# Two attentions of a streaming encoder: the two heads of a pair issued in turn, with one pair of logits ahead of the transposes

## The chip, the cores and the metric

The kernel runs on one core of one Trainium2 chip. The metric is the device time of one execution in microseconds (us). The core has five engines with instruction streams of their own, which meet only through semaphores: TensorE (PE in the profile, with PEld for its weight loads) does matmuls and transposes and writes to PSUM; VectorE (DVE) and ScalarE (ACT) read PSUM and do elementwise work and reductions; GpSimd (POOL) does elementwise work in SBUF; SyncE (SP) issues the loads.

## The reference

Two layers of an encoder are applied to a prompt of 512 frames and to a sample of 32 frames with 256 cached ones; the width is 1024. Layer 0 mixes by two gated recurrences, layer 1 by two attentions of 8 heads of 64 each: a forgetting attention (FoX) with causal masking and a decay added to the logits, and an attention over the keys that an indexer selects (DSA, 2 key heads shared by 4 query heads each). Each layer ends in a gated feed-forward network.

```python
def fox_attention(q, k_all, v_all, logf_all, q_start):
    ...
    def block(args):
        qb, cqb, pb = args
        logits = jnp.einsum('bqhd,bshd->bhqs', qb, k_all).astype(F32) * (hd ** -0.5)
        logits = logits + cqb.transpose(0, 2, 1)[..., None] - cum_t[:, :, None, :]
        logits = jnp.where(key_pos[None, None, None, :] <= pb[None, None, :, None], logits, -jnp.inf)
        p = jax.nn.softmax(logits, axis=-1)
        return jnp.einsum('bhqs,bshd->bqhd', p.astype(v_all.dtype), v_all)
...
def dsa_attention(q, k_all, v_all, iq, iw, ik_all, q_start):
    ...
        score = jax.nn.relu(jnp.einsum('bqhd,bsd->bqhs', iqb, ik_all).astype(F32))
        score = jnp.einsum('bqhs,bqh->bqs', score, iwb.astype(F32)) * IDX_SCALE
        ...
        _, idx = lax.top_k(score, topk)
        ...
        logits = jnp.einsum('bqgnd,bqkgd->bqgnk', qg, k_sel).astype(F32) * (hd ** -0.5)
        logits = jnp.where(valid[:, :, None, None, :], logits, -jnp.inf)
        p = jax.nn.softmax(logits, axis=-1)
        o = jnp.einsum('bqgnk,bqkgd->bqgnd', p.astype(v_sel.dtype), v_sel)
...
def run_trunk(...):
    for layer in range(DEPTH):
        xn = rmsnorm(x, norm_mix[layer])
        ...
        x = x + y
        x = x + swiglu(rmsnorm(x, norm_ffn[layer]), ffn_w_in[layer], ffn_w_out[layer])
```

All inputs and outputs are float32.

## The kernel before

Nearly all of the program is weight streaming: `plan` cuts every weight matrix into chunks of 128x1024; SyncE loads them into four slots, ScalarE makes the high part (`w_hi`), GpSimd the low part (`w_lo`), and TensorE multiplies three products of high and low parts (`job`, `tm_section`). Activations lie transposed, features on the partitions and the 544 frames (512 and 32) along the free axis. The order of every engine's instructions is written out by hand in one function per engine.

The change touches the function `attention(dsa)` alone, which stands once in each of three engines' programs (ScalarE, TensorE, VectorE) and is called twice in each: `attention(0)` for FoX and, after five jobs for DSA's keys and queries, `attention(1)` for DSA. Selection is done by adding a mask of large negative numbers, so both attentions have the same form.

The work of an attention is cut into `groups`. Group x belongs to a head h = 2t+e. Heads 2t and 2t+1 are a pair: their queries `qT[:, t, :]` and (in FoX) keys lie in partitions 0 to 63 (e=0) and 64 to 127 (e=1) of the same tile. A head has three groups: the first holds two query tiles of 128 rows, with 128 and 256 keys, side by side in one PSUM bank; the second one query tile with 384 keys; the third one with 512. Two more groups hold the 32 sample frames, four heads each (`tiles` is None). NX = 26 groups in all.

For a group the engines do in turn:
- `masks` (TensorE): decay and causal mask, or the selection's mask, as bf16 matmuls into logits bank x % 4. It waits until the exponentials of group x-4 are done (`at_e`).
- `logits` (TensorE): query times key added on top, float32. Signals `at_l`.
- `maxima` (VectorE): the row maxima. Signals `at_mx`.
- `exps` (ScalarE): exponentials with row sums into `prob[:, x % 3]`. Signals `at_e`.
- `normalise` (VectorE): reciprocal of the sums and scaling. Signals `at_p`.
- `turn` (TensorE): transposes of 128x128 into bank 4 + x % 2. Signals `at_t`.
- `copies` (ScalarE): that bank into the SBUF buffer `pt[x % 2]`. It waits for `at_t` and, since the buffer must be free, for the values of group x-2 (`at_v`). Signals `at_c`.
- `values` (TensorE): value times transposed probabilities. Even heads give rows 0 to 63 and odd heads rows 64 to 127 of bank 6 or 7. Signals `at_v`.
- `outputs` (ScalarE, then VectorE): once per pair of heads, the result as high and low part.

Before the change TensorE's loop over x issues masks(x+3), turn(x), logits(x+3), values(x-1); ScalarE's issues exps(x+2), copies(x); VectorE's issues maxima(x+2), normalise(x+1). In `attention(0)` VectorE also has rounds of the indexer's search (`largest`, `replace`) between the groups x = 1 to 5. The two buffers of `pt` are shown as `m_only` and `arena` in the profile.

## Time and profile before

| | before |
|---|---|
| time, median of 3 runs | 1521.56 us (1519.2 to 1530.3) |
| span of the profiled execution | 1520.4 us |
| TensorE busy | 1467.3 us (97%) |
| VectorE busy | 557.5 us (37%) |
| ScalarE busy | 561.3 us (37%) |
| GpSimd busy | 518.1 us (34%) |
| attention(0), first mask to last value | 882.41 to 954.16 us |
| attention(1), first mask to last value | 987.73 to 1055.30 us |

The profiled execution has no time of its own beside its span; the median of the runs is 1.2 us above that span. A busy TensorE counts from a matmul's start to its modelled end, so the distance between the starts of consecutive blocks tells better than the durations what a block costs. PEclk is the granted clock of TensorE as a share of 2.4 GHz; it has two levels, 1.00 and 0.50.

### The profile page before, as it was taken

How to read it: one execution, taken by the hardware profiler on the slowest of the kernel's cores; microseconds unless marked ns; L12 is line 12 of the kernel's file. 1: busy time of each engine (PE TensorE's matmuls, PEld its weight loads, DVE VectorE, ACT ScalarE, POOL GpSimd, SP SyncE). 2: the span in 40 equal slices, each digit the busy share in tenths (PEclk: the TensorE clock that was granted, in tenths of full speed). 3: DMA queues.
4: the chain of work that ended last, by engine and by line, in shares of the span. 5: the costliest groups of instructions: out<-in, count | busy, mean ns of one | idle time of the engine just before them, and what ended most of it. 6: DMA issues, size and time to landing. Idle time of an engine off the chain costs nothing.

```text
span 1520.4 us, 27440 instructions
## 1 busy us (share of the span) xinstructions
PE 1467.3 (97%) x11103; PEld 1361.9 (90%) x11103; DVE 557.5 (37%) x1131; ACT 561.3 (37%) x907; POOL 518.1 (34%) x235
## 2 busy tenths in 40 slices
PE   4998999999999999999999999999999999999998
PEld 3777889899999999999988766957999999999997
DVE  5114536633421223122408975163343212221224
ACT  4424546444432233122464254153353323321222
POOL 1421212233644344434535210300334533443442
PEclk9999899999999999999999999999999999999999
DMA  4221122232323222322332320200223332232221
GB/s 141 84 70 45 44 60 59 64 105 77 93 87 111 69 83 86 108 69 66 95 95 70 85 58 1 70 8 15 77 77 97 97 97 70 83 110 70 80 73 59
DMA packets 208777, 114.37 MB, mean 75 GB/s; under 512 B 16693, under 2 KB 202937, under 8 KB 208697
## 3 DMA queue, kind: packets, MB, share of 16 engines
q1 hardware_dynamic: 203448, 109.50, 25.0%
q10 hardware_dynamic: 5248, 3.73, 0.8%
q8 instruction: 59, 0.97, 0.3%
q14 instruction: 22, 0.17, 0.0%
HBM read 107.26 MB, written 5.96 MB: 74 GB/s over the span
## 4 chain that ended last, share of the span: by engine, by line
PE 62%; issue 29%; POOL 7%; DVE 2%; ACT 0%; POOLq 0%; DVEq 0%; ACTq 0%
PE ps L966 52%; POOL w_lo L523 7%; PE ps L1061 4%; PE ps L1283 1%; PE ps L1317 1%; PE ps L1296 1%; PE ps L1266 0%; DVE arena L1732 0%; DVE arena L1751 0%; DVE arena L1768 0%; PE ps L1312 0%; PE ps L1413 0%; DVE m_only L1763 0%; PE ps L1209 0%; DVE arena L1871 0%
## 5 line engine op out<-in xcount | busy, mean ns | idle before, releaser
L523 POOL TENSOR_TENSOR w_lo<-w_raw,w_hi 128x1024 fp32r<-128x1024 f32 x202 | 498.6, 2472 | 964.0 <-ACT w_hi L583 964.0
L966 PE MATMUL ps<-x_hi,w_hi 128*128 128x272 f32 (+1 forms) x1952 | 411.8, 293 | 10.3 <-DVE arena L1592 6.1
L966 PE MATMUL ps<-x_hi,w_lo 128*128 128x272 f32 (+1 forms) x1952 | 408.4, 291 | 0.0
L966 PE MATMUL ps<-x_lo,w_hi 128*128 128x272 f32 (+1 forms) x1952 | 407.1, 290 | 0.0
L966 PEld LDWEIGHTS ps<-x_hi,w_hi 128*128 128x128 f32 (+1 forms) x1952 | 310.5, 190 | 17.6 <-issue 11.7
L966 PEld LDWEIGHTS ps<-x_lo,w_hi 128*128 128x128 f32 (+1 forms) x1952 | 310.4, 191 | 0.5
L966 PEld LDWEIGHTS ps<-x_hi,w_lo 128*128 128x128 f32 (+1 forms) x1952 | 308.3, 191 | 0.5
L583 ACT ACTIVATE w_hi<-w_raw 128x1024 fp32r<-128x1024 f32 x202 | 211.2, 1050 | 194.2 <-PE ps L966 144.5
L966 PE MATMUL ps<-o_hi,w_hi 128*128 128x272 f32 x960 | 200.1, 290 | 2.0 <-DVE arena L1651 1.1
L966 PE MATMUL ps<-o_hi,w_lo 128*128 128x272 f32 x960 | 199.8, 290 | 0.0
L966 PE MATMUL ps<-o_lo,w_hi 128*128 128x272 f32 x960 | 199.0, 289 | 0.0
L966 PEld LDWEIGHTS ps<-o_hi,w_hi 128*128 128x128 f32 x960 | 152.0, 190 | 2.6 <-issue 2.6
L966 PEld LDWEIGHTS ps<-o_lo,w_hi 128*128 128x128 f32 x960 | 151.9, 190 | 0.0
L966 PEld LDWEIGHTS ps<-o_hi,w_lo 128*128 128x128 f32 x960 | 150.8, 190 | 0.0
L639 ACT ACTIVATE o_hi<-arena 128x544 f32 x44 | 29.0, 658 | 197.2 <-DVE arena L1504 197.2
L1497 DVE TENSOR_TENSOR arena<-ps,rstd 128x544 f32<-128x544 f32 x44 | 31.9, 725 | 163.2 <-PE ps L966 150.3
L635 ACT ACTIVATE arena<-arena 128x544 f32<-128x544 f32 x44 | 29.0, 660 | 168.6 <-DVE arena L1497 168.6
L1519 DVE TENSOR_TENSOR xT<-ps,xT 128x544 f32 x32 | 23.2, 725 | 162.9 <-PE ps L966 162.9
L1504 DVE TENSOR_TENSOR arena<-arena,ps 128x544 f32<-128x544 f32 x44 | 31.7, 721 | 123.9 <-PE ps L966 123.7
L1061 PE MATMUL ps<-w_hi,x_hi 128*128 128x512 f32 (+3 forms) x160 | 64.5, 403 | 8.1 <-DVE x_lo L1442 5.2
L1061 PE MATMUL ps<-w_hi,x_lo 128*128 128x512 f32 (+3 forms) x160 | 63.8, 399 | 0.0
L1061 PE MATMUL ps<-w_lo,x_hi 128*128 128x512 f32 (+3 forms) x160 | 63.5, 397 | 0.0
(240 smaller groups left out, 1377.4 us busy)
## 6 DMA issues: line engine op xcount, KB each, us to landing
w_raw<-in_ffn_w_in SPq DMA_DIRECT2D x88, 512.0 KB, 3.8
w_raw<-in_ffn_w_out SPq DMA_DIRECT2D x32, 512.0 KB, 3.8
w_raw<-in_ab_w_in SPq DMA_DIRECT2D x28, 512.0 KB, 3.8
w_raw<-in_cd_w_in SPq DMA_DIRECT2D x13, 512.0 KB, 3.8
w_raw<-in_ffn_w_out SPq DMA_DIRECT2D x16, 384.0 KB, 3.3
w_raw<-in_ab_w_out SPq DMA_DIRECT2D x8, 512.0 KB, 3.5
arena<-in_x_prompt SPq DMA_DIRECT2D x4, 512.0 KB, 5.0
w_raw<-in_cd_w_in SPq DMA_DIRECT2D x8, 256.0 KB, 3.5
```

The lines of the kernel that those rows point to most:

```text
L523: pool.tensor_tensor(wl[:, s, :], raw[:, s, :], wh[:, s, :].bitcast(F32), ALU.subtract).then_inc(lo_done, 1)
L583: act.activation(wh[:, s, :], raw[:, s, :], ACT.Copy).then_inc(hi_done, 1)
L635: act.activation(fsig[:, k // 2, :], fg[:, k // 2, :], ACT.Sigmoid).then_inc(f_sig, 1)
L639: act.activation(oh[:, bass.ds(i * 2 + k // 2, 1), :], fh[:, k // 2:k // 2 + 1, :], ACT.Copy).then_inc(f_hi, 1)
L966: mm = pe.matmul(ps[0:M, b + h, 0:HALF], w[:, s, k * M:(k + 1) * M], xs[x][:, k, h * HALF:(h + 1) * HALF], start=(begin and k == ks[0] and ...
L1061: mm = pe.matmul(out, (xh, xl)[x][:, k, i * P:min(T, (i + 1) * P)], w[:, s, kk * N:(kk + 1) * N], start=(k == 0 and a == 0), stop=(k == KT ...
L1283: mm = pe.matmul(L[:, c:c + nk], q[:, i * P:(i + 1) * P], ks_[:, 0:nk], start=False, stop=True, skip_group_check=True)
L1296: mm = pe.transpose(ps[0:m, 4 + x % 2, c:c + P], prob[:, x % 3, c:c + m], ident[:, :])
L1317: mm = pe.matmul(out[:, i * P:(i + 1) * P], v[:, kb, vcol], pt[x % 2][:, c + kb * P:c + (kb + 1) * P], start=(kb == 0), stop=(kb == i), sk ...
L1497: dve.tensor_tensor(two(fgk), pair(g), two(rstd[:, :]), ALU.mult).then_inc(frees(g), 1)
L1504: dve.tensor_tensor(two(fh[:, k, :]), two(fgk), pair(u), ALU.mult).then_inc(frees(u), 1)
L1519: dve.tensor_tensor(xv, pair(c), xv, ALU.add).then_inc(frees(c), 1)
```

## The change

`groups` is ordered by shape first and head of the pair last, so that groups 2s and 2s+1 are the same shape of heads 2t and 2t+1. Each engine's loop runs over the NS = 13 pairs of groups s. `logits` and `values` take a pair and issue the two heads' matmuls in turn; `masks`, `turn`, `maxima`, `exps`, `normalise` and `copies` are unchanged and are called for one head and then the other. TensorE issues masks of pair s+1, turn of pair s, logits of s+1, values of s-1. PSUM banks and buffers are the same, and so is the number of matmuls.

```diff
@@ -431,10 +431,11 @@
         N_M0_OUT = sum(2 * (1 if kind == "a" else 2) for kind, _ in units)
 
 
-        groups = [(2 * t + e, tiles) for t in range(4) for e in range(2)
-                  for tiles in ([(0, 0, P), (1, P, 2 * P)], [(2, 0, 3 * P)], [(3, 0, 4 * P)])]
+        groups = [(2 * t + e, tiles) for t in range(4)
+                  for tiles in ([(0, 0, P), (1, P, 2 * P)], [(2, 0, 3 * P)], [(3, 0, 4 * P)]) for e in range(2)]
         groups += [(w, None) for w in range(2)]
         NX = len(groups)
+        NS = NX // 2
         pairs_end = [6 * (t + 1) - 1 for t in range(4)] + [NX - 1]
         block = ctx.enter_context(nc.Block())
 
@@ -860,13 +861,15 @@
 
                 exps(0)
                 exps(1)
-                for x in range(NX + 2):
-                    if x + 2 < NX:
-                        exps(x + 2)
-                    if x < NX:
-                        copies(x)
-                    if x - 2 in pairs_end:
-                        outputs(x - 2)
+                for s in range(NS + 1):
+                    for x in (2 * s, 2 * s + 1):
+                        if s < NS:
+                            copies(x)
+                    if 2 * s - 1 in pairs_end:
+                        outputs(2 * s - 1)
+                    for x in (2 * s + 2, 2 * s + 3):
+                        if x < NX:
+                            exps(x)
 
             hp[0] = C_M1 + LEAD
             for c in range(C_M1, C_M1 + 4):
@@ -1267,22 +1270,28 @@
                                 mm = pe.matmul(L[:, o + i * P:o + nk], identb[:, :], caus, start=False, stop=False, skip_group_check=True)
                     mm.then_inc(at_m, 1)
 
-                def logits(x):
-                    h, tiles = groups[x]
-                    L = ps[:, x % 4, :]
-                    pe.wait_ge(at_m, X0 + x + 1)
-                    for k, t, e, ks_, kc_, _, o in heads_of(x):
-                        q = qT[e * HD:(e + 1) * HD, t, :]
-                        if tiles is None:
-                            pe.matmul(L[o:o + 32, 0:PAST], q[:, TP:T], kc_, start=False, stop=True, skip_group_check=True,
-                                      tile_position=(e * HD, o))
-                            mm = pe.matmul(L[o:o + 32, PAST:KS], q[:, TP:T], ks_[:, TP:T], start=False, stop=True,
-                                           skip_group_check=True, tile_position=(e * HD, o))
-                        else:
-                            for i, c, nk in tiles:
-                                mm = pe.matmul(L[:, c:c + nk], q[:, i * P:(i + 1) * P], ks_[:, 0:nk], start=False, stop=True,
-                                               skip_group_check=True)
-                    mm.then_inc(at_l, 1)
+                def logits(s):
+
+                    pe.wait_ge(at_m, X0 + 2 * s + 2)
+                    tiles = groups[2 * s][1]
+                    if tiles is None:
+                        for x in (2 * s, 2 * s + 1):
+                            L = ps[:, x % 4, :]
+                            for k, t, e, ks_, kc_, _, o in heads_of(x):
+                                q = qT[e * HD:(e + 1) * HD, t, :]
+                                pe.matmul(L[o:o + 32, 0:PAST], q[:, TP:T], kc_, start=False, stop=True, skip_group_check=True,
+                                          tile_position=(e * HD, o))
+                                mm = pe.matmul(L[o:o + 32, PAST:KS], q[:, TP:T], ks_[:, TP:T], start=False, stop=True,
+                                               skip_group_check=True, tile_position=(e * HD, o))
+                            mm.then_inc(at_l, 1)
+                        return
+                    for i, c, nk in tiles:
+                        for x in (2 * s, 2 * s + 1):
+                            (k, t, e, ks_, _, _, _), = heads_of(x)
+                            mm = pe.matmul(ps[:, x % 4, c:c + nk], qT[e * HD:(e + 1) * HD, t, i * P:(i + 1) * P], ks_[:, 0:nk],
+                                           start=False, stop=True, skip_group_check=True)
+                            if i == tiles[-1][0]:
+                                mm.then_inc(at_l, 1)
 
                 def turn(x):
 
@@ -1296,40 +1305,50 @@
                         mm = pe.transpose(ps[0:m, 4 + x % 2, c:c + P], prob[:, x % 3, c:c + m], ident[:, :])
                     mm.then_inc(at_t, 1)
 
-                def values(x):
-
-                    pi = [n for n, last in enumerate(pairs_end) if x <= last][0]
+                def values(s):
+
+                    x0 = 2 * s
+                    pi = [n for n, last in enumerate(pairs_end) if x0 <= last][0]
                     if pi + PX >= 2:
                         pe.wait_ge(at_o, PX + pi - 1)
-                    pe.wait_ge(at_c, X0 + x + 1)
-                    tiles = groups[x][1]
-                    for k, t, e, _, _, vcol, o in heads_of(x):
-                        out = ps[e * HD:(e + 1) * HD, 6 + (PX + pi) % 2, :]
-                        if tiles is None:
-                            for kb in range(3):
-                                vv = v[0:TS, NT, vcol] if kb == 2 else vc_[:, kb, vcol]
-                                m = TS if kb == 2 else P
-                                mm = pe.matmul(out[:, t * TS:(t + 1) * TS], vv, pt[x % 2][0:m, kb * P + o:kb * P + o + TS],
-                                               start=(kb == 0), stop=(kb == 2), skip_group_check=True)
-                        else:
-                            for i, c, nk in tiles:
-                                for kb in range(i + 1):
-                                    mm = pe.matmul(out[:, i * P:(i + 1) * P], v[:, kb, vcol], pt[x % 2][:, c + kb * P:c + (kb + 1) * P],
-                                                   start=(kb == 0), stop=(kb == i), skip_group_check=True)
-                    mm.then_inc(at_v, 1)
-
-                for x in range(3):
-                    masks(x)
-                    logits(x)
-                for x in range(NX + 1):
-                    if x + 3 < NX:
-                        masks(x + 3)
-                    if x < NX:
-                        turn(x)
-                    if x + 3 < NX:
-                        logits(x + 3)
-                    if x >= 1:
-                        values(x - 1)
+                    pe.wait_ge(at_c, X0 + x0 + 2)
+                    bank = 6 + (PX + pi) % 2
+                    tiles = groups[x0][1]
+                    if tiles is None:
+                        for x in (x0, x0 + 1):
+                            for k, t, e, _, _, vcol, o in heads_of(x):
+                                for kb in range(3):
+                                    vv = v[0:TS, NT, vcol] if kb == 2 else vc_[:, kb, vcol]
+                                    m = TS if kb == 2 else P
+                                    mm = pe.matmul(ps[e * HD:(e + 1) * HD, bank, t * TS:(t + 1) * TS], vv,
+                                                   pt[x % 2][0:m, kb * P + o:kb * P + o + TS],
+                                                   start=(kb == 0), stop=(kb == 2), skip_group_check=True)
+                            mm.then_inc(at_v, 1)
+                        return
+                    for i, c, nk in tiles:
+                        for kb in range(i + 1):
+                            for x in (x0, x0 + 1):
+                                (k, t, e, _, _, vcol, _), = heads_of(x)
+                                mm = pe.matmul(ps[e * HD:(e + 1) * HD, bank, i * P:(i + 1) * P], v[:, kb, vcol],
+                                               pt[x % 2][:, c + kb * P:c + (kb + 1) * P],
+                                               start=(kb == 0), stop=(kb == i), skip_group_check=True)
+                                if i == tiles[-1][0] and kb == i:
+                                    mm.then_inc(at_v, 1)
+
+                masks(0)
+                masks(1)
+                logits(0)
+                for s in range(NS + 1):
+                    if s + 1 < NS:
+                        masks(2 * s + 2)
+                        masks(2 * s + 3)
+                    if s < NS:
+                        turn(2 * s)
+                        turn(2 * s + 1)
+                    if s + 1 < NS:
+                        logits(s + 1)
+                    if s >= 1:
+                        values(s - 1)
 
             def turn_keys(src, base):
 
@@ -1806,23 +1825,20 @@
                         b = b[:, 0:4 * TS].rearrange("p (t n) -> p t n", t=4)
                     dve.tensor_tensor(o, b, hh.bitcast(F32), ALU.subtract).then_inc(at_o, 1)
 
-                maxima(0)
-                maxima(1)
-                normalise(0)
-                for x in range(NX + 3):
-
-                    late = 3 if not dsa and 1 <= x <= LATE else None
+                for s in range(NS + 2):
+
+                    late = 3 if not dsa and 1 <= s <= LATE else None
                     if late is not None:
                         largest(late)
-                    if x + 2 < NX:
-                        maxima(x + 2)
-                    if x + 1 < NX:
-                        normalise(x + 1)
-                    if x - 3 in pairs_end:
-                        outputs(x - 3)
+                    for step in (maxima, normalise):
+                        for x in (2 * s, 2 * s + 1):
+                            if s < NS:
+                                step(x)
+                    if 2 * s - 3 in pairs_end:
+                        outputs(2 * s - 3)
                     if late is not None:
                         replace(late)
-                        if x == LATE:
+                        if s == LATE:
                             chosen(late)
 
             LATE = 5
```

TensorE around the middle of attention(0), before, two groups of one head (384 and 512 keys). L1266 and L1267 are masks, L1296 transposes of the group before, L1283 logits, L1317 values:

```order
L1266 MATMUL ps<-arena 128x384
L1267 MATMUL ps<-arena,identb 128x128
L1296 MATMUL ps<-ident,arena 128x128 x3
L1283 MATMUL ps<-arena 128x384
L1317 MATMUL ps<-m_only,arena 64x128 x3
L1266 MATMUL ps<-arena 128x512
L1267 MATMUL ps<-arena,identb 128x128
L1296 MATMUL ps<-ident,arena 128x128 x4
L1283 MATMUL ps<-arena 128x512
L1317 MATMUL ps<-arena 64x128 x3
```

The same place in the changed kernel: masks (L1269, L1270) of both heads, transposes (L1305) of the pair before, logits (L1291) of both heads, values (L1332) in turn:

```order
L1269 MATMUL ps<-arena 128x384
L1270 MATMUL ps<-arena,identb 128x128
L1269 MATMUL ps<-arena 128x384
L1270 MATMUL ps<-arena,identb 128x128
L1305 MATMUL ps<-ident,arena 128x128 x6
L1291 MATMUL ps<-arena 128x384 x2
L1332 MATMUL ps<-arena 64x128
L1332 MATMUL ps<-m_only,arena 64x128
L1332 MATMUL ps<-arena 64x128
L1332 MATMUL ps<-m_only,arena 64x128
L1332 MATMUL ps<-arena 64x128
L1332 MATMUL ps<-m_only,arena 64x128
```

Before, the transposes ahead of a group's logits belong to a group two places earlier than the last logits issued; now they belong to the pair whose logits were issued last, and the values that follow belong to the pair before that one.

ScalarE at the same stage, before. L848 are copies, L832 exponentials, L856 outputs; the names in brackets are the semaphores that an instruction waits for (att_values is `at_v`, att_turned `at_t`, att_max `at_mx`):

```order
L848 ACTIVATE arena<-ps 128x384 [waits att_values,att_turned]
L832 ACTIVATE arena,small<-ps,small 128x384 [waits att_turned,att_max]
L848 ACTIVATE m_only<-ps 128x512 [waits att_values,att_turned]
L832 ACTIVATE arena,small<-ps,small 128x512 [waits att_turned,att_max]
L848 ACTIVATE arena<-ps 128x384 [waits att_values,att_turned]
L832 ACTIVATE arena,small<-ps,small 128x128 [waits att_turned,att_max]
L832 ACTIVATE arena,small<-ps,small 128x256
L848 ACTIVATE m_only<-ps 128x384 [waits att_values,att_turned]
L856 ACTIVATE o_hi<-ps 128x512 [waits att_values]
```

And in the changed kernel (L849 copies, L833 exponentials, L857 outputs):

```order
L849 ACTIVATE arena<-ps 128x512 [waits att_values,att_turned]
L849 ACTIVATE m_only<-ps 128x512 [waits att_values,att_turned]
L833 ACTIVATE arena,small<-ps,small 128x128 [waits att_turned,att_max]
L833 ACTIVATE arena,small<-ps,small 128x256
L833 ACTIVATE arena,small<-ps,small 128x128 [waits att_turned,att_max]
L833 ACTIVATE arena,small<-ps,small 128x256
L849 ACTIVATE arena<-ps 128x384 [waits att_values,att_turned]
L849 ACTIVATE m_only<-ps 128x384 [waits att_values,att_turned]
L857 ACTIVATE o_hi<-ps 128x512 [waits att_values]
L833 ACTIVATE arena,small<-ps,small 128x384 [waits att_turned,att_max] x2
L849 ACTIVATE arena<-ps 128x384 [waits att_values,att_turned]
L849 ACTIVATE m_only<-ps 128x384 [waits att_values,att_turned]
```

Copies and exponentials alternated by group; now two copies stand ahead of the exponentials of the next pair. The copies' wait for att_values was for values that TensorE issued ahead of that group's transposes; now it is for values that TensorE issues behind the next pair's logits.

## Rows read from the trace of the kernel before

**Rows 1.** The page: busy us (share of the span) and instructions of each engine.

```profile
PE 1467.3 (97%) x11103; PEld 1361.9 (90%) x11103; DVE 557.5 (37%) x1131; ACT 561.3 (37%) x907; POOL 518.1 (34%) x235
```

**Rows 2.** Windows by stage: length, busy us (instructions) of PE, PEld, DVE, ACT, POOL; PEclk.

```profile
882.41:954.16 71.75, 71.58 (x471) 45.29 (x471) 40.91 (x140) 35.40 (x101) 0.00 (x0) 0.98 0.05 17
...
987.73:1055.30 67.57, 66.63 (x430) 42.19 (x431) 37.08 (x125) 34.78 (x102) 0.00 (x0) 0.99 0.02 5
```

**Rows 3.** Timeline of PE, one head in attention 0: start, us, instructions.

```profile
901.45 0.92 PE L1283 MATMUL ps<-arena 64*128 64x128 f32 x4
902.30 1.09 PE L1317 MATMUL ps<-m_only,arena 128*64 128x128 f32 x8
...
903.98 0.91 PE L1283 MATMUL ps<-arena 64*128 64x384 f32 x2
904.82 0.87 PE L1317 MATMUL ps<-arena 128*64 128x128 f32 x6
...
905.90 0.60 PE L1296 MATMUL ps<-ident,arena 128*128 128x128 f32 x4
906.44 1.12 PE L1283 MATMUL ps<-arena 64*128 64x512 f32 x2
```

**Rows 4.** Windows of one head's cycle in each stage, columns as in rows 2.

```profile
900.73:908.29 7.56, 7.56 (x47) 4.72 (x47) 4.68 (x16) 4.22 (x12) 0.00 (x0) 1.00 0.01 2
1005.31:1012.62 7.31, 7.31 (x44) 4.57 (x43) 4.61 (x15) 4.21 (x12) 0.00 (x0) 1.00 0.00 1
```

**Rows 5.** Timeline of PE, the indexer's scores.

```profile
824.22 1.99 PE L1224 MATMUL ps<-arena 64*128 64x512 f32 x8
```

**Rows 6.** Timeline of PE, state updates with two heads and with one.

```profile
126.66 2.59 PE L1117 MATMUL ps<-arena 32*64 32x128 f32 x64
...
217.01 2.81 PE L1117 MATMUL ps<-arena 32*128 32x128 f32 x32
```

**Rows 7.** Timeline of DVE in attention 0.

```profile
907.60 0.69 DVE L1784 TENSOR_REDUCE small<-ps 128x1 f32<-128x512 f32 x1 [0.66 <-PE ps L1283]
...
908.58 0.42 DVE L1794 TENSOR_SCALAR arena<-arena,small 128x384 f32<-128x384 f32 x1
...
910.70 0.15 DVE L1791 RECIPROCAL small<-small 128x1 f32<-128x1 f32 x1
910.89 0.49 DVE L1794 TENSOR_SCALAR arena<-arena,small 128x512 f32<-128x512 f32 x1
...
913.34 0.55 DVE L1794 TENSOR_SCALAR arena<-arena,small 128x128 f32<-128x128 f32 x2
```

**Rows 8.** Timeline of ACT in attention 0.

```profile
908.51 0.69 ACT L832 ACTIVATE arena<-ps,small 128x512 f32<-128x512 f32 x1 [1.37 <-DVE small L1786]
909.09 0.19 ACT L832 ACTIVATION_READ_ACCUMULATOR arena<-ps,small 128x1 f32 x1
...
910.83 0.37 ACT L832 ACTIVATE arena<-ps,small 128x128 f32<-128x128 f32 x1 [1.16 <-DVE small L1786]
...
911.54 0.20 ACT L832 ACTIVATION_READ_ACCUMULATOR arena<-ps,small 128x1 f32 x1
911.64 0.49 ACT L848 ACTIVATE arena<-ps 128x384 f32<-128x384 f32 x1
...
913.27 0.59 ACT L832 ACTIVATE arena<-ps,small 128x384 f32<-128x384 f32 x1 [1.13 <-DVE small L1786]
...
914.10 0.60 ACT L848 ACTIVATE m_only<-ps 128x512 f32<-128x512 f32 x1 [0.17 <-PE ps L1296]
```

**Rows 9.** Windows around two falls of the clock, columns as in rows 2.

```profile
149.00:153.00 4.00, 1.71 (x14) 1.46 (x13) 1.63 (x3) 3.16 (x11) 0.00 (x0) 1.00 0.14 33
153.00:156.00 3.00, 3.00 (x15) 3.00 (x15) 0.38 (x1) 2.97 (x7) 0.00 (x0) 0.50 0.00 0
835.70:842.50 6.80, 6.06 (x14) 4.37 (x15) 6.70 (x26) 2.29 (x3) 4.71 (x2) 0.50 0.22 59
843.00:849.00 6.00, 6.00 (x28) 4.57 (x26) 5.29 (x17) 1.06 (x1) 1.35 (x1) 1.00 0.43 89
```

## The prediction

> **What bounds the kernel now.** I read the page's line of busy times first: TensorE is busy 1467.3 of 1520.4 us, VectorE and ScalarE 37% each [rows 1]. So the question is what the change does to TensorE's time, and only in the two attention stages, since everything else keeps its instructions. The windows by stage say that attention 0 takes 71.75 us and attention 1 takes 67.57, TensorE busy in 71.58 and 66.63 of them, VectorE in 40.91 and 37.08, ScalarE in 35.40 and 34.78 [rows 2]. The stages are bound by TensorE's own stream. The two steady cycles say the same: one head costs 7.56 us in attention 0 and 7.31 in attention 1, with TensorE busy throughout [rows 4]. A pair of heads therefore costs 15.12 and 14.62.
>
> The timeline of such a cycle gives the blocks [rows 3]. I call the three query groups of a head A (two tiles, 128 and 256 keys), B (384 keys) and C (512). Logits take .85 in A and .84 in B (start to next start); in C a span of 1.12, less the .07 by which a span overlaps what follows, so 1.05. Values take .87 until done, 1.09 in C (.80 and 1.02 of TensorE's time). Transposes take .54 in C, which has four, and an estimated .43 in A and B, which have three. Per head that is 2.74 for logits, 2.62 for values and 1.40 for transposes; the remaining .80 of 7.56 are masks (.55 of 7.31 in attention 1).
>
> **Part 1: pairs of matmuls.** The logits of a head contract over 64 partitions, the even head's in the lower half and the odd head's in the upper, and now follow each other tile by tile. The indexer's scores already stand so: four 64x128 matmuls of 512 columns, halves alternating, take 1.99 us [rows 5], where one alone takes 1.12 [rows 3]. So two run at once and a pair costs what one does. The values fill 64 columns of the array, even and odd head in different ones. The recurrence shows that case: 64 records of 64 columns, two heads alternating, take 2.59; 32 records of 128 columns take 2.81 [rows 6]. So these double up too. The saving on TensorE's stream is 2.74+2.62 = 5.36 per pair of heads, and with eight pairs in both stages 42.9 us. The sample groups keep their order within a head.
>
> The Trainium skill, "TensorE: Matmul & The Clock Gate", Part 3 (Packing small matmuls), gives 3.07x for four row tiles, some 77% of ideal. By it a pair would cost 1.3 times one, and TensorE's saving would shrink to an estimated 30 us. The rows here show the full factor of two, so they decide.
>
> **Part 2: the order, and what is late next.** TensorE's order is now: masks of pair s+1, transposes of pair s, logits of s+1, values of s-1. Before, logits ran three groups ahead of the transposes and the softmax of a group was hidden behind two others. Now the logits of s+1 stand behind both transposes of s, and these wait for the softmax of s. Only values and masks lie between.
>
> A second wait makes it longer. ScalarE copies the transposes of s out (`copies`) only once the values of s-1 are done, since they free that buffer; those values now stand behind the logits of s+1. On ScalarE the exponentials of s+1 are queued behind these copies. TensorE, in turn, waits for those exponentials through `normalise`. So a closed chain sets each step: logits(s+1), values(s-1), two copies of s, two groups of exponentials of s+1, the last normalise, the last transposes of s+1, next logits. The maxima of s+1 on VectorE run beside values and copies and are hidden (less than 1.7 us for two groups, against 1.7 to 2.4 of cover).
>
> The prices, from the timelines of VectorE and ScalarE: a wait between engines .04 (logits end at 906.44+1.12, the maximum starts at 907.60) [rows 3, 7]. Reciprocal to scaling .19, scaling .49 in C, .42 in B, .55 in A, with two waits: .76, .69, .82 [rows 7]. Exponentials to the end of the read-out: .91 in A, with the next ScalarE operation .81 after the start; .67 and .57 in B; .77 and .67 in C [rows 8]; B's read-out is taken as C's, .08 beyond the activation's end. A copy takes .49 (.60 in C), the next operation starting .10 before its end, as there [rows 8].
>
> A step in which the logits are A's, behind copies of C and values of B: .85 logits + .87 values + .04 + 1.00 copies + .81+.91 exponentials + .82 normalise + .43 transposes = 5.73. With B's logits: .84 + 1.09 + .04 + .78 + .50 (the pair's `outputs`, which stands there on ScalarE, priced as a copy of 512) + .57+.67 + .69 + .43 = 5.61. With C's: 1.05 + .87 + .04 + .78 + .67+.77 + .76 + .54 = 5.48. A pair of heads costs 16.8 us, against 15.12 and 14.62 now. That is +1.7 and +2.2, four times each: +15.6. Filling the pipe costs an estimated 1.5 more in both stages together: the masks of two heads stand ahead of the first logits, and the first softmax has nothing beside it. The ends, with the sample groups, I take as equal. VectorE's extra search rounds in attention 0 (`largest`, `replace`) and its `outputs` fall into the transposes and logits of the next pair and cost nothing; should they not fit, each costs under .5 us, at most 4 in all. The 42.9 us saved on TensorE turn into waiting. Sum of this part: **+17 us, 1539**. Bounds: if half of my .5 for `outputs` and the .10 overlaps are off, 4 us either way; I keep 1534 to 1544.
>
> **Part 3: the clock.** In such a step TensorE now stands idle, in one piece from the masks to the first transposes: in A .04+1.00+.91+.82, less some .6 of masks and overlap, 2.2 us; in B 2.1; in C 1.75; and again up to .4 between the two transposes. The trace has an idle piece of this kind: between 149 and 153 us TensorE is busy 1.71 of 4.00 us, and behind it the granted clock is .50, 1.2 instead of 2.4 GHz, though TensorE is then busy without a gap [rows 9]. The same matmuls take 6.06/14 = .43 us at .50 and 6.00/28 = .21 at 1.00 [rows 9]: half the clock doubles their time. In the closed chain TensorE's blocks are 2.74+2.83+1.40 = 7.0 per pair of heads, so at half clock the pair costs 7.0 more; were all eight pairs at half, 56. Neither bound is excluded: 0 (the clock holds, as with TensorE busy now, 1.00 [rows 4]) and 56. I take a third, +19: my idle pieces of 2.1 and 2.2 are near the row's 2.29 but under it, each is followed by two to three us of dense work, and a lower clock fills the idle pieces itself.
>
> **Sum.** The profiled execution's span is 1520.4; the median of three runs is 1521.56 (1519.2 to 1530.3), 1.2 more, and I add to the median: 1521.6 + 17 + 19 = **1558 us**.
>
> **Rivals.**
> 1. The clock holds. Then 1539. For it: idle never exceeds what I worked out, and no row shows 2.2 us followed by dense work. Against it: [rows 9]. Chance .20; a third of it lies within 1% of now.
> 2. TensorE stays the bound, as its stream alone suggests: 1521.6 - 42.9 = 1479. VectorE (2x4.68 = 9.4 us per pair) and ScalarE (2x4.22) [rows 4] would fit beside TensorE's 15.12-5.36 = 9.8. This is the faster side: one mechanism, the work of s-1 covering the whole softmax of s. It decides where values and masks last as long as two softmaxes, that is 1.4 us against some 3.7, which is why I give it .05. The Trainium skill, "TensorEngine Tiling (Array Packing)", PSUM Bottleneck, warns that after such a speedup the engines that empty PSUM may bind. By busy time, as that rule reads, they would not bind here and this rival's 1479 would stand; the trace lets me read latency instead.
> 3. The copies don't hold up the exponentials, because the wait on the values costs less than I think. Then exponentials start behind the maxima, some .9 us after the logits, not 1.7 to 2.4: 3.2 less per pair of heads, 25 in all, 1513. Within 1%. Against it stands ScalarE's fixed order. Chance .10.
> 4. The pairs don't run at once, so the change doesn't do what it says. Then each step grows by its logits and values, 5.4 per pair of heads, 43 in all: 1582 at full clock. Against it: [rows 5, 6]. Chance .05.
>
> The forecast itself has .60. The range reaches down to rival 1's lower bound, and up to the clock at half for two thirds of the steps, 1521.6+17+37 = 1576: 1531 to 1578 leaves out about 2 in 10. A measurement of this kernel tells a change from none at about 1%, 15 us. Faster .05; within it .10 + .07 = .17; slower .78.
>
> **What the changed profile would show.** Part 1: two heads' logits of 512 keys in about 1.1 us, starts in twos. Part 2: TensorE's busy share in both stages near 60%, stages of 85 to 95 us; TensorE waiting before the transposes for VectorE's normalise, ScalarE's copies starting at the end of the values. Part 3: granted clock of the stages near .85. I would be wrong if the logits of s+1 start before the transposes of s, if the steps at full clock are far from 5.6 us, or if the clock falls for most of both stages.

## The result, and the profile after

| | before | changed |
|---|---|---|
| time, median of 5 runs each | 1530.3 us (1519.2 to 1537.2) | 1576.62 us (1569.49 to 1580.27) |
| changed / before, 95% interval | | 1.0308 (1.0249 to 1.0367) |
| span of the profiled execution | 1520.4 us | 1567.8 us |
| mean granted clock of it | 0.981 | 0.958 |
| attention 0 | 71.75 us | 96.05 us |
| attention 1 | 67.57 us | 94.94 us |

The change costs 3.1%. By the profiled spans it is 47.4 us: the stages grow by 24.30 + 27.37 = 51.7, and everything outside them is 4.3 shorter. The profiled execution of the changed kernel is the fastest of its five. One of the ten runs of e7 below took 6036 us, four times the others, and isn't in e7's ratio.

The page of the changed kernel: the line of busy times, which answers to [rows 1], and the granted clock in 40 equal slices.

```profile
PE 1459.9 (93%) x11099; PEld 1352.6 (86%) x11103; DVE 561.4 (36%) x1131; ACT 557.3 (36%) x907; POOL 519.3 (33%) x235
...
PEclk9999899999999999999999877977899999999999
```

The windows of the changed kernel: first the two stages, which answer to [rows 2], then four steps in attention 0, each from the start of one pair's logits to the start of the next. Columns as in [rows 2]; the granted clock is the first number behind POOL's.

```profile
877.35:973.40 96.05, 70.42 (x471) 42.55 (x471) 42.14 (x140) 33.17 (x101) 0.00 (x0) 0.77 0.04 13
1006.70:1101.64 94.94, 65.02 (x427) 40.00 (x431) 38.01 (x125) 32.65 (x102) 0.00 (x0) 0.76 0.01 4
...
895.41:902.92 7.51, 5.15 (x31) 3.15 (x30) 3.96 (x16) 2.69 (x10) 0.00 (x0) 0.73 0.00 0
902.92:910.27 7.35, 5.29 (x31) 3.02 (x30) 3.41 (x12) 2.48 (x7) 0.00 (x0) 0.73 0.01 2
910.27:917.37 7.10, 5.37 (x33) 2.94 (x32) 4.17 (x13) 2.21 (x6) 0.00 (x0) 0.74 0.00 0
930.94:936.60 5.66, 3.92 (x33) 2.28 (x33) 2.95 (x9) 2.21 (x6) 0.00 (x0) 0.98 0.02 4
```

VectorE and ScalarE have as much to do as before. TensorE isn't busy throughout any more, and in most steps its clock is at the low level for about half the time (.77 and .76 on average, so 46% and 48% of the stages). The three such steps shown take 7.1 to 7.5 us, the one that stands almost wholly at the high level 5.66. That step can be followed on three engines. Its timeline (start, us, engine, line, idle time before and what ended it) begins with the logits of a pair with 512 keys and ends with the next logits.

```profile
930.94 1.13 PE L1291 MATMUL ps<-arena 64*128 64x512 f32 x4
932.00 0.32 PE L1332 MATMUL ps<-arena 128*64 128x128 f32 x1
932.01 0.32 PE L1332 MATMUL ps<-m_only,arena 128*64 128x128 f32 x1
...
932.60 0.27 PE L1332 MATMUL ps<-m_only,arena 128*64 128x128 f32 x1
932.81 0.23 PE L1269 MATMUL ps<-arena 96*128 96x128 bf16 x1
...
932.97 0.49 ACT L849 ACTIVATE arena<-ps 128x384 f32<-128x384 f32 x1 [3.21 <-PE ps L1332]
933.35 0.48 ACT L849 ACTIVATE m_only<-ps 128x384 f32<-128x384 f32 x1
933.73 0.69 ACT L833 ACTIVATE arena<-ps,small 128x512 f32<-128x512 f32 x1
...
934.96 0.22 ACT L833 ACTIVATION_READ_ACCUMULATOR arena<-ps,small 128x1 f32 x1
935.21 0.16 DVE L1810 RECIPROCAL small<-small 128x1 f32<-128x1 f32 x1
935.28 1.39 PE L1305 MATMUL ps<-ident,arena 128*128 128x128 f32 x8 [1.73 <-DVE arena L1813]
935.41 0.49 DVE L1813 TENSOR_SCALAR arena<-arena,small 128x512 f32<-128x512 f32 x1
936.60 0.59 PE L1291 MATMUL ps<-arena 64*128 64x128 f32 x2
```

This is the closed chain of the prediction, with nothing between its links: logits 1.06 (930.94 to 932.00), values .87 (to 932.87), a wait of .10, two copies .76 (932.97 to 933.73), two exponentials 1.45 (to 935.18), the last normalise .72 (to 935.90), the last transposes .70 (to 936.60). The sum is 5.66. Two heads' logits of 512 keys take 1.06 together, where one head's took 1.05 [rows 3]. The values of two heads take .81 to the next block's start, where one head's took .80.

The waits of the changed kernel over both stages, of PE and of ACT (us in total, times, longest):

```profile
PE ps L1305 <- DVE arena L1813: 50.7, 28, 2.4
...
ACT arena L849 <- PE ps L1332: 95.8, 22, 5.3
```

TensorE waits before its transposes for VectorE's normalise, ScalarE before its copies for TensorE's values.

### The profile page after: what moved, and what is told of

It is laid out like the page before. It is cut to its first block, busy times and chain, and to the rows that moved or that the text cites. A ratio compares the mean times of both kernels' runs of the same rounds, so it can differ in the third digit from the quotient of the medians.

```text
span 1567.8 us, 27416 instructions
## 1 busy us (share of the span) xinstructions
PE 1459.9 (93%) x11099; PEld 1352.6 (86%) x11103; DVE 561.4 (36%) x1131; ACT 557.3 (36%) x907; POOL 519.3 (33%) x235
## 4 chain that ended last, share of the span: by engine, by line
PE 59%; issue 30%; POOL 7%; DVE 3%; ACT 2%; POOLq 0%; ACTq 0%; DVEq 0%
PE ps L969 51%; POOL w_lo L524 6%; PE ps L1064 4%; PE ps L1291 1%; PE ps L1305 1%; PE ps L1332 1%; ACT arena L833 1%; PE ps L1323 0%; PE ps L1432 0%; DVE arena L1751 0%; DVE arena L1770 0%; DVE arena L1813 0%; DVE arena L1787 0%; DVE m_only L1782 0%; ACT m_only L849 0%
## 5 line engine op out<-in xcount | busy, mean ns | idle before, releaser
L1305 PE MATMUL ps<-ident,arena 128*128 128x128 f32 (+1 forms) x172 | 38.4, 368 | 50.9 <-DVE arena L1813 50.7
L1305 PEld LDWEIGHTS ps<-ident,arena 128*128 128x128 f32 (+1 forms) x172 | 24.5, 179 | 65.7 <-DVE arena L1813 65.5
```

The costliest lines, as they stand in the source:

```text
L1305: mm = pe.transpose(ps[0:m, 4 + x % 2, c:c + P], prob[:, x % 3, c:c + m], ident[:, :])
```

## The experiments

Ten kernels ran. "Stages" are the lengths of attention 0 and attention 1 in the profiled execution, with the granted clock of each.

| kernel | time, us | ratio to before, 95% | stages, us | clock |
|---|---|---|---|---|
| before | 1530.3 | 1 | 71.75 + 67.57 = 139.3 | .98, .99 |
| changed | 1576.62 | 1.0308 (1.0249 to 1.0367) | 96.05 + 94.94 = 191.0 | .77, .76 |
| e1_not_in_turn | 1579.76 | 1.0347 (1.0300 to 1.0393) | 95.74 + 97.73 = 193.5 | .79, .77 |
| e2_filler | 1546.22 | 1.0135 (1.0088 to 1.0182) | 80.83 + 80.52 = 161.4 | .99, .98 |
| e3_logits_first | 1531.98 | 1.0023 (0.9998 to 1.0049) | 75.70 + 69.81 = 145.5 | .86, .95 |
| e4_lead | 1501.65 | 0.9846 (0.9797 to 0.9894) | 63.00 + 55.53 = 118.5 | .91, .97 |
| e5_free_copies_filler | 1523.09 | 0.9973 (0.9945 to 1.0000) | 71.17 + 69.82 = 141.0 | .98, .98 |
| e6_values_first_filler | 1543.05 | 1.0107 (1.0074 to 1.0140) | 80.80 + 79.98 = 160.8 | .97, .96 |
| e7_lead_apart | 1543.83 | 1.0080 (1.0047 to 1.0113) | 83.36 + 76.86 = 160.2 | .87, .92 |
| e8_lead_values_between | 1555.0 | 1.0179 (1.0130 to 1.0228) | 86.25 + 86.56 = 172.8 | .83, .81 |
| e9_between_copies_first | 1523.34 | 0.9970 (0.9943 to 0.9997) | 69.29 + 68.43 = 137.7 | .96, .94 |
| e10_lead_masks_early | 1502.81 | 0.9851 (0.9808 to 0.9894) | 60.13 + 58.44 = 118.6 | .96, .90 |

Each ratio is against runs of the kernel before on the same chip (medians 1525.6 to 1530.3). The stages are those of one execution each. What lies outside them is the same work in all twelve kernels, yet it takes between 1376.8 us (changed) and 1386.3 (e3), so a difference of a few us between two kernels may come from the execution and not from the kernel.

The theory behind the first four: the loss is a closed chain (logits of s+1 issued behind the transposes of s), plus the low clock that its idle pieces bring; the pairing itself works. The rivals: the pairs don't run at once, or the clock is no part of it.

### e1: the two heads one after the other

```diff
-                    for i, c, nk in tiles:
-                        for x in (2 * s, 2 * s + 1):
+                    for x in (2 * s, 2 * s + 1):
+                        for i, c, nk in tiles:
...
-                    for i, c, nk in tiles:
-                        for kb in range(i + 1):
-                            for x in (x0, x0 + 1):
+                    for x in (x0, x0 + 1):
+                        for i, c, nk in tiles:
+                            for kb in range(i + 1):
```

> The changed kernel with one part undone: the two heads of a pair keep their common place in the order, but the tiles of the even head are issued before those of the odd head, in logits and in values. My theory: no two matmuls run at once any more, and logits and values of both heads lie on the closed chain, so each pair of heads takes 5.4 us longer, 43 us in all at full clock. TensorE is then busy in a larger share of the stage, so the clock should fall less often than in the changed kernel, which gives some of it back: 20 to 43 us above the changed kernel, ratio to before 1.045 to 1.06. Rival (pairs never ran at once, or the pairing isn't on the path): within 5 us of the changed kernel, ratio 1.03.

The expectation failed. The stages are 2.5 us longer, not 20 to 43, and the two intervals of the ratio overlap. The timeline of PE in this kernel shows a values block, six records of the even head (operand in `arena`) and then six of the odd head (`m_only`) as issued:

```profile
946.58 0.54 PE L1332 MATMUL ps<-arena 128*64 128x128 f32 x3
946.86 0.32 PE L1332 MATMUL ps<-m_only,arena 128*64 128x128 f32 x1
946.96 0.27 PE L1332 MATMUL ps<-arena 128*64 128x128 f32 x1
947.01 0.27 PE L1332 MATMUL ps<-m_only,arena 128*64 128x128 f32 x1
...
947.23 0.49 PE L1332 MATMUL ps<-m_only,arena 128*64 128x128 f32 x3
947.66 0.34 PE L1269 MATMUL ps<-arena 96*128 96x384 bf16 x1
```

The first record of the odd head starts .28 behind the even head's first, ahead of three that were issued before it. The block takes 1.08 (946.58 to 947.66), against .81 with the heads in turn and 1.6 for two single blocks of .80 [rows 3]. So the two heads still run mostly at once, although they don't alternate in the program. Logits with 384 or 512 keys have one tile per head, so there the edit changes nothing. Those of 128 and 256 keys have two, and this block takes .86 here (945.72 to 946.58) as in the changed kernel. The Trainium skill, "TensorE: Matmul & The Clock Gate", Part 2 (Step-by-step), says that only weight loads are pulled ahead and that matmuls stay in program order. These rows show starts out of the order in which the kernel issues them, and the measurement decides. e1 therefore doesn't price the pairing. It shows that the grouping does most of the work. The strict turn is worth .27 us in such a values block, an estimated 6.5 over the 24 blocks of both stages; 2.5 were measured, in stages whose clock was slightly higher (.79 and .77 against .77 and .76).

### e2: work for TensorE's idle piece

```diff
                     if s < NS:
+                        if s:
+                            pe.wait_ge(at_c, X0 + 2 * s - 1)
+                        for _ in range(6):
+                            pe.matmul(ps[:, 4, :], identb[0:96, :], sel[0:96, 0:4, :], start=True, stop=True, skip_group_check=True)
                         turn(2 * s)
```

The six added matmuls write to a bank that the transposes overwrite.

> The changed kernel plus six bf16 matmuls of 512 columns (about 1.3 us at full clock) per pair of groups, put on TensorE where it sits idle ahead of the transposes; they write the transposes' bank, which is overwritten at once, and their result is used by nothing. My theory: half of the loss is the clock, which falls because TensorE idles 2 us per step. With the idle time filled the granted clock in both attention stages is 0.95 or more, each stage takes 78 to 83 us, and although work was added the kernel gets 25 to 35 us faster than the changed one, ratio to before 1.005 to 1.015. Rival (the chain of waits alone makes the loss, the clock is its harmless companion): no faster than the changed kernel, ratio 1.03 or more.

Windows of this kernel, the two stages and one pair of heads in three steps:

```profile
884.78:965.61 80.83, 71.27 (x548) 39.40 (x548) 42.15 (x140) 33.18 (x101) 0.00 (x0) 0.99 0.04 15
999.69:1080.21 80.52, 68.16 (x509) 36.21 (x509) 37.91 (x125) 32.65 (x102) 0.00 (x0) 0.98 0.02 4
...
917.46:923.29 5.83, 4.77 (x37) 2.56 (x36) 3.02 (x13) 2.69 (x10) 0.00 (x0) 1.00 0.00 0
923.29:928.99 5.70, 5.07 (x37) 2.55 (x37) 2.97 (x9) 2.48 (x7) 0.00 (x0) 1.00 0.01 3
928.99:934.59 5.60, 5.29 (x40) 2.79 (x39) 2.95 (x9) 2.21 (x6) 0.00 (x0) 1.00 0.00 1
```

As expected: more work makes the kernel 1.7% faster. The clock holds and the stages are 191.0 - 161.4 = 29.6 us shorter: that was the clock's share. What is left over before, 161.4 - 139.3 = 22.0, is the chain at full clock. Its steps are 5.83, 5.70 and 5.60 where the prediction had 5.73, 5.61 and 5.48. The added matmuls don't lengthen it by what can be seen: the step with 512 keys takes 5.60 here against 5.66 without them, and the transposes still wait for VectorE, 13.9 us in 31 pieces:

```profile
PE ps L1305 <- DVE arena L1817: 13.9, 31, 0.9
```

The Trainium skill, "TensorE: Matmul & The Clock Gate", Part 1 (A second HAM failure mode), tells of a kernel in which short and frequent idling between groups of matmuls makes the clock swing between its levels. The trace agrees: .73 in steps with idle pieces of about 2 us (50.7 us in 28 pieces over both stages), 1.00 with the same steps filled.

### e3: logits ahead of the transposes

```diff
-                    if s < NS:
-                        turn(2 * s)
-                        turn(2 * s + 1)
                     if s + 1 < NS:
                         logits(s + 1)
+                    if s < NS:
+                        turn(2 * s)
+                        turn(2 * s + 1)
```

> The changed kernel with TensorE's loop in another order: logits of pair s+1 ahead of the transposes of pair s, nothing else moved. My theory: the logits leave the closed chain, whose steps become 4.8, 4.4 and 4.9 us instead of 5.6, 5.5 and 5.7, so 2.7 us less per pair of heads and 22 in all at full clock; idle pieces shrink to about 1.4 us and the clock falls seldom. Ratio to before 0.99 to 1.01, stages of 68 to 75 us. Rival (lookahead of logits doesn't matter, ScalarE's hold on the values is the whole cost): no gain, 1.03.

The ratio is as expected, but no more than even with before. This one move gives back 191.0 - 145.5 = 45.5 of the 51.7 us. Attention 0 is just over the 68 to 75 us expected, and there the clock didn't hold as I had thought (.86). TensorE still waits 27.8 us before the transposes in both stages, in 31 pieces. ScalarE's queue still has the copies of s ahead of the exponentials of s+1; e3 alone doesn't show that this is the reason.

### e5 and e6: the second wait, apart from the clock

e5 is the changed kernel with four buffers for the copied transposes, so that `copies` waits for values two pairs back, and with four filler matmuls a step in place of e2's six. e6 is e2 with values ahead of logits.

```diff
-                    if x >= 2:
-                        act.wait_ge(at_v, X0 + x - 1)
+                    if x >= 4:
+                        act.wait_ge(at_v, X0 + x - 3)
```

> The filled kernel of the second experiment (changed kernel, clock held by added matmuls; here four instead of six per pair, since less idle time is left) with four SBUF buffers for the copied transposes instead of two, so that ScalarE's copies of pair s no longer wait for the values of s-1. My theory of two waits in one closed chain: the exponentials then start behind the maxima, the steps become 4.8, 4.8 and 4.8 us instead of 5.7, 5.6 and 5.5, so 2.4 us less per pair of heads, 19 in all: stages near 71 us, ratio to before 1.00 (1.0135 for the filled kernel). Rival (ScalarE's hold is hidden, the softmax's own length sets the step): no gain, 1.01 or more.

> The filled kernel of the second experiment with the values of s-1 ahead of the logits of s+1 on TensorE. The copies' wait is then over early, but the values stand on the chain themselves. My theory: steps of 5.6, 5.1 and 5.6 us, 0.5 less per pair of heads, 4 in all: ratio 1.01. Rival (ScalarE's hold on the values alone is the cost, wherever the values stand): the same gain as with four buffers, 19 us, ratio 1.00.

Both ratios are as expected. Freeing the copies takes 161.4 - 141.0 = 20.4 us from the stages (19 expected), and a pair of heads costs 14.83 us (logits from 912.44 to 927.27) instead of 17.13. So ScalarE's wait for the values was a real link. Putting the values first merely moves them from one place in the chain to another: 160.8 against 161.4, where 4 us less had been expected.

### e4 and e7: a full pair of lead, with the heads together and apart

e4 issues masks(s+1), logits(s+1), values(s-1), transposes of s. ScalarE issues exponentials of x+2 and copies of x in turn, VectorE normalise(x) and maxima(x+2), and `prob` has four buffers.

```diff
+                    if s + 1 < NS:
+                        logits(s + 1)
+                    if s >= 1:
+                        values(s - 1)
                     if s < NS:
                         turn(2 * s)
                         turn(2 * s + 1)
-                    if s + 1 < NS:
-                        logits(s + 1)
-                    if s >= 1:
-                        values(s - 1)
...
                     for x in (2 * s, 2 * s + 1):
+                        if x + 2 < NX:
+                            exps(x + 2)
                         if s < NS:
                             copies(x)
```

> Pairs in turn with a full lookahead: TensorE issues masks and logits of s+1, values of s-1, then the transposes of s; ScalarE alternates exponentials of s+1 and copies of s; VectorE alternates normalise of s and maxima of s+1; a fourth buffer for the probabilities in a region that is free there. My theory: no chain closes within a step, and the stage is bound by TensorE (9.8 us per pair of heads in attention 0, 9.3 in attention 1) or VectorE (9.4) with little idle time, so 10 to 11 us per pair against 15.1 and 14.6 before: 30 to 40 us faster than before, ratio 0.975 to 0.98, clock 0.95 or more in the stages. Rival (pairing cannot pay because VectorE and ScalarE bind): 12 us or more per pair, ratio 0.985 or above.

e7 is e4 with logits of the even head, values of the even head, logits of the odd head, values of the odd head:

```diff
-                    if s + 1 < NS:
-                        logits(s + 1)
-                    if s >= 1:
-                        values(s - 1)
+                    for e in range(2):
+                        if s + 1 < NS:
+                            logits(s + 1, e)
+                        if s >= 1:
+                            values(s - 1, e)
```

> The full lookahead of the fourth experiment with the heads kept apart: logits of the even head, values of the even head, logits of the odd head, values of the odd head. Order of everything else, buffers and waits are the same. My theory: neighbours on TensorE now share rows or columns of the array and can't run at once, so the stage loses the 5.4 us per pair of heads and is bound by TensorE at about 16 us per pair: 35 to 43 us above the full lookahead, ratio to before 1.005 to 1.015. Rival (TensorE finds partners several places away, or the pairing gives little): within 10 us of the full lookahead.

Windows of e4: the stages, one pair of heads of attention 0 in three steps, and one whole pair in each stage. Below them whole pairs of e7:

```profile
880.38:943.38 63.00, 55.59 (x471) 36.04 (x471) 42.44 (x148) 34.02 (x101) 0.00 (x0) 0.91 0.05 19
976.12:1031.65 55.53, 47.48 (x431) 30.52 (x431) 35.73 (x125) 33.36 (x102) 0.00 (x0) 0.97 0.02 6
...
903.94:908.11 4.17, 3.45 (x32) 2.32 (x32) 3.96 (x17) 2.51 (x11) 0.00 (x0) 1.00 0.00 0
908.11:911.69 3.58, 3.43 (x31) 2.10 (x32) 3.33 (x13) 2.59 (x9) 0.00 (x0) 1.00 0.00 0
911.69:915.49 3.80, 3.53 (x31) 2.11 (x31) 2.54 (x7) 2.58 (x8) 0.00 (x0) 1.00 0.01 2
...
900.14:911.68 11.54, 10.40 (x92) 6.52 (x92) 10.65 (x38) 7.67 (x25) 0.00 (x0) 1.00 0.01 1
993.22:1003.85 10.63, 9.74 (x85) 6.05 (x85) 8.31 (x29) 7.63 (x24) 0.00 (x0) 1.00 0.01 2
```

```profile
930.92:946.49 15.57, 15.17 (x93) 9.75 (x93) 8.62 (x29) 7.71 (x25) 0.00 (x0) 1.00 0.01 2
1044.67:1059.99 15.32, 14.67 (x83) 9.19 (x84) 8.62 (x29) 7.70 (x24) 0.00 (x0) 1.00 0.00 0
```

e4 beats both kernels: 1.5% under before. A pair of heads costs 11.54 us in attention 0 (11.00 the pair behind it, 911.68 to 922.68) and 10.63 in attention 1, against 15.12 and 14.62 before and 17.13 in e2. That is inside the 10 to 11 expected in attention 1 and over it in attention 0, where the clock was also lower than expected (.91). The ratio .9846 is over the .975 to .98 expected and on the edge of the rival's .985, so the rival, that VectorE and ScalarE bind, isn't out for attention 0: VectorE, with the rounds of the search, is busy 10.65 of the 11.54 us of the pair shown. In attention 1 it is busy 8.31 of 10.63, and TensorE 9.74.

e7 is the price of the pairing where it can show, and is as expected: stages 160.2 against 118.5, 41.7 us more. Some of it is the clock again (.87 and .92 against .91 and .97). At full clock a pair of heads costs 15.57 and 15.32 in e7, with TensorE busy in 15.17 and 14.67 of it. That is 4.0 to 4.6 and 4.7 more than in e4, an estimated 35 to 37 for eight pairs, where the prediction had 5.36 each and 42.9 in all on TensorE's stream.

### e8 and e9: values between masks and logits

e8 is e4 with the values ahead of the logits; e9 is e8 with ScalarE's order as in the changed kernel, both copies and then both exponentials.

```diff
e8, on e4:
-                    if s + 1 < NS:
-                        logits(s + 1)
                     if s >= 1:
                         values(s - 1)
+                    if s + 1 < NS:
+                        logits(s + 1)
e9, on e8:
                     for x in (2 * s, 2 * s + 1):
-                        if x + 2 < NX:
-                            exps(x + 2)
                         if s < NS:
                             copies(x)
...
+                    for x in (2 * s + 2, 2 * s + 3):
+                        if x < NX:
+                            exps(x)
```

> The full lookahead with the values of s-1 between masks and logits of s+1. In the full lookahead the logits wait 0.22 us for the masks just ahead of them, at every step; now the values cover that. My theory: 0.22 x 24 = 5 us less than the full lookahead, ratio 0.981. Rival (VectorE is the bound there by now): no change, 0.985.

That failed by 3.7%: e8 is 53 us slower than e4. The timeline of ACT in e8, in a step from logits at 909.88 to logits at 915.28, shows why; below it the first values and the next logits on PE:

```profile
911.95 0.69 ACT L833 ACTIVATE arena<-ps,small 128x512 f32<-128x512 f32 x1 [2.45 <-DVE small L1804]
...
912.63 0.48 ACT L849 ACTIVATE arena<-ps 128x384 f32<-128x384 f32 x1
913.27 0.69 ACT L833 ACTIVATE arena<-ps,small 128x512 f32<-128x512 f32 x1 [0.15 <-DVE small L1804]
...
913.94 0.48 ACT L849 ACTIVATE m_only<-ps 128x384 f32<-128x384 f32 x1
...
914.48 0.32 PE L1331 MATMUL ps<-arena 128*64 128x128 f32 x1 [0.86 <-ACT m_only L849]
...
915.28 0.38 PE L1290 MATMUL ps<-arena 64*128 64x128 f32 x2
```

Both copies of s (L849) stand behind exponentials of s+1 (L833), and those wait for the maxima of logits issued at 909.88. The values of s start at 914.48 behind the second copy, and the next logits behind them. The chain is closed again in another place: logits, maxima, exponential, copy, exponential, copy, values, logits, 5.40 us. In e4 the values stand behind the next logits, so the late copy holds nobody. e9 was made to test this.

> The kernel of e8_lead_values_between with one edit: ScalarE issues both copies of pair s (and the pair's outputs) ahead of both exponentials of s+1, instead of in turn with them. Theory: e8 was slow because TensorE's logits(s+1) stand behind values(s-1), these wait for the second copy of s-1, and that copy stands on ScalarE behind two groups of exponentials, the later ones of logits just issued; the trace of e8 shows the closed loop logits 909.88, maxima 911.04, exponentials 911.95, copy 912.63, exponentials 913.27, copy 913.94, values 914.48. With the copies first the loop opens: values wait for two copies alone (about 1.1 us behind the transposes, .6 of it beside masks), and the next loop is two copies, two exponentials, normalise, transposes, 1.0 + 1.6 + .8 + .5 = 3.9 to 4.3 us a step instead of 5.4. That is 12 to 13 per pair of heads against e8's 16, some 28 us less plus what the clock gives back (e8 had it low for 62 us of the two stages): 1510 to 1525 with the kernel before at 1527, ratio .99 to 1.00. Rival: values ahead of logits is itself the cost (logits wait for values whatever ScalarE's order is); then the ratio stays at 1.01 to 1.02 as in e8.

The ratio is as expected: ScalarE's order alone takes 172.8 - 137.7 = 35.1 us from the stages. A pair of heads costs 13.86 (912.68 to 926.54), over the 12 to 13 expected. The rival as stated, that e8's loss comes from values ahead of logits whatever ScalarE's order is, is out. But e9 is still 137.7 - 118.5 = 19.2 us behind e4, from which it differs in two things, the place of the values and ScalarE's order. Which of them costs this, no run separates. In attention 0 ScalarE's copies wait 15.5 + 11.9 us for the transposes in e9 and 2.8 in e4.

### e10: masks a pair earlier

```diff
                     if s >= 1:
                         values(s - 1)
+                    if s + 2 < NS:
+                        masks(2 * s + 4)
+                        masks(2 * s + 5)
                     if s < NS:
                         turn(2 * s)
```

> The kernel of e4_lead with one edit: the masks go one pair further ahead. TensorE issues logits(s+1), values(s-1), masks(s+2), transposes of s, with four groups of masks ahead of the loop. In e4 each step has .28 us from the last masks record to the first logits, which wait for the masks' own semaphore, against .06 between masks records: .22 times 24 steps is 5.3 us. Here values and transposes lie between. Expected .978 to .983 of the kernel before (e4: .985); masks(s+2) need the exponentials of s, which the transposes of s need anyway, so no new wait. Rival: the .28 is covered anyway because transposes then wait for normalise; then the ratio stays at .985.

No gain: 118.6 against 118.5. The rival holds, with another releaser than it named. Waits of e10 over both stages, and below them those of e4:

```profile
PE ps L1331 <- ACT m_only L849: 11.3, 20, 1.3
...
PE ps L1304 <- DVE arena L1812: 1.2, 3, 0.6
```

```profile
PE ps L1304 <- DVE arena L1812: 6.8, 12, 1.9
PE ps L1331 <- ACT m_only L849: 4.3, 9, 1.3
```

The time that logits no longer wait for masks is waited by the values (L1331) for ScalarE's second copy. The two lines add up to 11.1 in e4 and 12.5 in e10. By stage the kernels differ, 60.13 and 58.44 against 63.00 and 55.53, and the clock goes with it (.96 and .90 against .91 and .97). What bounds e4 wasn't isolated: TensorE is busy 90% and 92% of the two pairs of heads shown, VectorE 92% of the one in attention 0, and TensorE's waits for ScalarE's copies and VectorE's normalise are those 11.1 us of 118.5.

## Why the prediction came out as it did

The forecast was 1558 within 1531 to 1578, from 1521.56. Measured was 1576.62, with the kernel before at 1530.3 in the same comparison; as a ratio 1.024 was forecast and 1.031 measured. So the time lies only 1.4 us under the top of the range, and of the 18.6 us above the forecast 8.7 are the higher median of the kernel before. The sign and the mechanism were right. Of the size, two terms were too small and one, small itself, was missing (measured by the profiled executions, rounded):

| term | forecast | measured | from |
|---|---|---|---|
| chain at full clock | +17 | +22.0 | e2's stages less before's |
| clock | +19 | +29.6 | changed stages less e2's |
| outside the stages | 0 | -4.3 | spans less stages |
| sum | +36 | +47.4 | |

**Part 1, the pairs.** Right: two heads' logits take 1.06, two heads' values .81. That TensorE's saving turns wholly into waiting was right for this order. e7 against e4 shows that the saving is there once the order lets it through. I took strict alternation for the condition; e1 shows that standing next to each other is enough for most of it.

**Part 2, the chain.** Right link by link. The step with 512 keys is 5.66 against 5.48. Two links were short: the wait between the values and the copies (.10, not .04) and the last transposes with the wait ahead of them (.70, not .54). The others are within .04. By e2, a pair of heads costs 17.13 in both stages where 16.8 was forecast, so the eight pairs cost 4 x 2.01 + 4 x 2.51 = 18.1 instead of 15.6. The other 3.9 of the 22.0 are what is left, and so lie outside the steady pairs, in filling and emptying the pipe, priced at 1.5: the ends, which I took as equal, seem not to be. That is worked out by subtraction, no run isolates it. e5 confirms the second wait: without it a pair costs 2.3 less, where rival 3 had put 3.2. Rival 3 itself is out.

**Part 3, the clock.** The step that was mis-sized. The sentence that failed is that a third of the bound of 56 would be lost because my idle pieces are near [rows 9] but under it, and because a lower clock fills them. They were long enough: TensorE waited 50.7 us before its transposes in 28 pieces, about the 48 of the prediction (6.05 for each of eight pairs), and the clock fell in nearly every step and came back in the next. 29.6 of 56 is a half. The trace of the kernel before could have said more than the one row I used: it has TensorE idle for 2.29 us at 149.6 and again at 197.9, 2.31 at 291.8, 2.47 at 181.5 and 2.90 at 833.5, and each time the clock falls to its low level in that piece or less than 3 us behind it. Of shorter pieces, 1.27 us at 111.6 has such a fall behind it, 1.90 at 138.3 and 1.59 at 371.0 have none. Two of the falls, as windows (columns as in [rows 2]):

```profile
201.00:204.00 3.00, 3.00 (x15) 3.00 (x14) 0.22 (x2) 2.94 (x8) 0.00 (x0) 0.50 0.01 3
296.40:299.00 2.60, 2.60 (x13) 2.38 (x12) 1.68 (x5) 0.00 (x0) 0.84 (x1) 0.50 0.24 73
```

A lower clock does fill the idle pieces, the clock then rises, and the next idle piece brings it down again; so the loss settles between the bounds, nearer the middle. That last sentence is how I read the steps above, not something that a run isolates. The share of time at the low clock, 46% and 48%, stayed just under the "most of both stages" that would have proved me wrong.

**Outside the stages** the changed kernel is 4.3 us shorter. The mean clocks .981 and .958 and the stages' own say that TensorE was at the low clock for an estimated 53 us outside the stages before and 42 after. Half of that difference is 5 to 6 us, which is enough. But the twelve profiled executions differ by 9.5 us outside the stages, so the 4.3 may be no effect of the change at all.

**The rivals.** That the clock holds (1539) is what e2 makes by force: 1546. That TensorE stays the bound (1479) would need a deeper lead than the change has. Even e4, with a full pair of lead, gets 1501.65 and costs 11.54 per pair in attention 0, not 9.8. That the pairs don't run at once was excluded by the first step read. Of the signs, the stages (85 to 95 foreseen) are 96.05 and 94.94, and the clock (.85 foreseen) is .77 and .76. The busy share was to be near 60% and reads 73% and 68%. Matmuls at the low clock last twice as long, but that isn't all of it: the step at the high level is also busy 3.92 of 5.66 us, 69%.

## What to carry to other kernels

When an engine gets faster by running two things at once, look first for the work that its queue puts between an operand's request and its use. Here moving the logits of s+1 ahead of the transposes of s got back to even (e3), and only the kernels with a full pair of lead on all three engines were clearly faster than before (e4 and e10). Write the closed chain down link by link across all queues, and do it again for each reordering, the other engines' orders included; e8 lost 53 us against e4 by moving one call. And price TensorE's idle pieces at both clock levels: the low clock cost 29.6 us here, more than the 22.0 of the closed chain itself, and six matmuls of no use in each idle piece bought 1.7%.

## What the hardware showed that I had not expected

- Matmuls of two heads in different column halves of the array start out of the order in which they were issued: the odd head's first .28 us behind the even head's first, ahead of three issued before it. Their block takes 1.08 us against .81 in turn and 1.6 for two blocks one after the other (e1, the changed kernel and [rows 3]).
- In the changed kernel the granted clock alternates between its two levels through both stages, .77 and .76 on average. The steps with .72 to .74 are 7.1 to 7.6 us, where the steps at full clock are 5.60 to 5.83 (e2).
